# Order of work at the seams of a four-layer mixer kernel: output chunks one unit ahead, first scores inside the last projection unit, signals per bank

## Time and profile before

| | us |
|---|---|
| median of three runs | 2666.73 |
| profiled execution | 2667.27 |
| its span | 2665.3 |
| TensorE busy | 2569.6 (96%) |
| VectorE busy | 1645.6 (62%) |
| ScalarE busy | 1178.4 (44%) |
| GpSimd busy | 310.4 (12%) |
| mean granted TensorE clock | 0.989 of full speed |

### The profile page before, as it was taken

The page is one execution under the profiler, slowest core; times in us unless marked ns, Lnnn a source line. Parts: engine busy times, 40 slices in busy tenths (PEclk is TensorE's granted clock), DMA queues, the critical chain, the costliest instruction groups (busy, mean ns, idle before and its releaser), DMA issues.

```text
span 2665.3 us, 38269 instructions
## 1 busy us (share of the span) xinstructions
PE 2569.6 (96%) x13432; PEld 2165.7 (81%) x13432; DVE 1645.6 (62%) x2865; ACT 1178.4 (44%) x1819; POOL 310.4 (12%) x258
## 2 busy tenths in 40 slices
PE   8999999999999799999999899999999999999997
PEld 6889978888878577888878778888879998788886
DVE  7578567774252957667356667664375784776733
ACT  4367454443232745444235454442333773544421
POOL 1001121110010001111010021110010110211100
PEclk9999999999999999999999999999999999999999
DMA  4410023333233012332322023233333001233331
GB/s 157 135 33 1 1 95 103 94 96 101 74 112 96 9 56 81 101 95 79 114 73 72 32 80 102 95 94 97 98 97 112 14 2 40 80 102 96 94 98 53
DMA packets 61907, 210.90 MB, mean 79 GB/s; under 512 B 8528, under 2 KB 10320, under 8 KB 61776
## 3 DMA queue, kind: packets, MB, share of 16 engines
q1 hardware_dynamic: 61776, 209.13, 24.9%
HBM read 207.01 MB, written 2.10 MB: 78 GB/s over the span
## 4 chain that ended last, share of the span: by engine, by line
PE 86%; DVE 11%; ACT 1%; issue 1%; DMA 0%; DVEq 0%; SPq 0%; ACTq 0%
PE psum L304 20%; PE psum L305 20%; PE psum L306 20%; PE psum L1066 6%; PE psum L1056 3%; PE psum L902 2%; PE psum L904 2%; PE psum L903 2%; DVE left L1986 2%; PE psum L1046 2%; PE psum L1045 2%; DVE xl L477 2%; DVE h L494 1%; PE psum L338 1%; DVE share L1992 1%
## 5 line engine op out<-in xcount | busy, mean ns | idle before, releaser
L304 PE MATMUL psum<-xh,w_hi 128*128 128x512 f32 x1712 | 671.1, 392 | 18.2 <-DVE w_lo L266 13.5
L305 PE MATMUL psum<-xh,w_lo 128*128 128x512 f32 x1712 | 669.5, 391 | 0.0
L306 PE MATMUL psum<-xl,w_hi 128*128 128x512 f32 x1712 | 669.1, 391 | 0.0
L266 DVE TENSOR_TENSOR w_lo<-w_raw,w_hi 128x1024 fp32r<-128x1024 f32 x226 | 279.0, 1250 | 516.4 <-ACT w_hi L260 515.1
L260 ACT ACTIVATE w_hi<-w_raw 128x1024 fp32r<-128x1024 f32 x226 | 235.0, 1056 | 570.0 <-PE psum L306 448.7
L304 PEld LDWEIGHTS psum<-xh,w_hi 128*128 128x128 f32 x1712 | 323.4, 189 | 87.2 <-issue 14.6
L306 PEld LDWEIGHTS psum<-xl,w_hi 128*128 128x128 f32 x1712 | 323.5, 189 | 67.7
L305 PEld LDWEIGHTS psum<-xh,w_lo 128*128 128x128 f32 x1712 | 323.7, 189 | 66.8
L698 DVE TENSOR_TENSOR w_lo<-w_raw,w_hi 128x1024 fp32r<-128x1024 f32 x160 | 209.3, 1308 | 253.6 <-ACT w_hi L694 253.6
L304 PE MATMUL psum<-ah,w_hi 128*128 (+1 forms) x704 | 273.9, 389 | 0.0
L305 PE MATMUL psum<-ah,w_lo 128*128 (+1 forms) x704 | 273.9, 389 | 0.0
(11 more groups left out here) (197 smaller groups left out, 3836.7 us busy)
## 6 DMA issues: line engine op xcount, KB each, us to landing
w_raw<-w_up SPq DMA_DIRECT2D x176, 512.0 KB, 3.6
w_raw<-w_down SPq DMA_DIRECT2D x88, 512.0 KB, 3.6
w_raw<-nsa_in SPq DMA_DIRECT2D x56, 512.0 KB, 4.1
w_raw<-sb_in SPq DMA_DIRECT2D x24, 512.0 KB, 3.6
w_raw<-nsa_out SPq DMA_DIRECT2D x16, 512.0 KB, 3.6
w_raw<-swa_in SPq DMA_DIRECT2D x10, 512.0 KB, 3.9
w_raw<-sb_out SPq DMA_DIRECT2D x8, 512.0 KB, 3.6
w_raw<-swa_out SPq DMA_DIRECT2D x8, 512.0 KB, 3.6
```

Source lines behind the costliest of these rows:

```text
L266: nc.vector.tensor_tensor(w_lo[:, u % RING, :], w_raw[:, u % RING, :], w_hi[:, u % RING, :].bitcast(F32), ALU.subtract).then_inc(split_don ...
L304: nc.tensor.matmul(bank(p, o), wh[:, k, o, :], xhi(k), start=(first and k == 0), stop=False)
L305: nc.tensor.matmul(bank(p, o), wl[:, k, o, :], xhi(k), start=False, stop=False)
L306: mm = nc.tensor.matmul(bank(p, o), wh[:, k, o, :], xlo(k), start=False, stop=(last and k == 1))
```

## The change

1. In `dve_nsa`, the second flat subtraction moves behind two weight splits and the gate copy.
2. In `pe_nsa`, products and transposes of the compressed branch are placed anew between the window units; the first four scores stand in the middle of the last window unit. A new semaphore `wk_done` tells DVE when the window keys alone are whole. DVE copies them after the first four biased tiles, ACT the window values after the second exponential. All four query operands are made ahead on ACT.
3. In `pe_out`, chunks 4 and 5 are turned before unit 1, and 6 and 7 before unit 2; on ACT and DVE one weight split stands behind chunk 1 and one behind chunk 5 (nsa and swa).
4. In `pe_sb`, the scores of tiles 0 to 3 stand before the last value unit, whose products are ordered by bank; `sv_done` signals each bank, `sv_free` each copy of one; one weight split moves behind the sigmoids and scans of tiles 0 and 1.

```diff
@@ kv_panel
                     for o in range(2):
-                        three(bank(p, o), ...
+                        mm = three(bank(p, o), ...
+                    if keys is not None and c == DC - 1:
+                        mm.then_inc(keys, 1)
@@ dve_k
-            dve.wait_ge(units_done, u_end)
+            if b:
+                dve.wait_ge(wk_done, nsa_before[l] + 1)
+            else:
+                dve.wait_ge(units_done, u_end)
@@ pe_attention, values(s)
+                    if kind == "nsa" and it == 0 and s == 0:
+                        pe.wait_ge(evac_s, s_after[plan.mix_p[l] + 7])
@@ dve_attention, ahead()
                 queries(0, 1)
-                if late and kind == "nsa":
-                    late()
                 for s in range(4):
                     biased(0, s)
                 if kind == "nsa":
+                    late()
                     queries(0, 2)
@@ act_attention, turn() and ahead()
                     exps(s)
+                    if kind == "nsa" and it == 0 and s == 1:
+                        late()
...
-                queries(0, 0)
-                queries(0, 1)
-                if late and kind == "nsa":
-                    late()
-                    queries(0, 2)
-                    queries(0, 3)
+                for r in range(R if kind == "nsa" else 2):
+                    queries(0, r)
@@ act_turn_o (and the same with split_lo behind dve_turn_o in dve_nsa and dve_swa)
                 nc.scalar.activation(xh[:, c, :], turn_bank(l, c), ACT.Copy).then_inc(oh_done, 1)
+                if c in (1, 5):
+                    split_hi(act, plan.out_u[l] + c // 4 + AHEAD)
@@ pe_out
-                if j >= 2:
-                    pe_turn_o(pe, l, 2 * j)
-                    pe_turn_o(pe, l, 2 * j + 1)
+                if j < 3:
+                    pe_turn_o(pe, l, 2 * j + 2)
+                    pe_turn_o(pe, l, 2 * j + 3)
                 pe.wait_ge(o_ready, 8 * l + 2 * j + 2)
@@ act_out and dve_out (done = 2 in nsa and swa)
-            split_his(act, u, 6)
+            split_his(act, u + done, 6 - done)
@@ pe_nsa
-            window(2, turn_late)
-            mixed(0)
+            window(2, mix_first)          # mixed(0), turned(2), turned(3)
             mixed(1)
-            window(3, mix_late)
-            pe.wait_ge(co_ready, TC * (k + 1))
-            pe.wait_ge(k_ready, kr_before[l] + 2)
-            pe.wait_ge(v_ready, kvs_before[l] + 1)
-            ...
+            mixed(2)
+            mixed(3)
+
+            def last_unit(first_scores):
+                def begin():
+                    pe.wait_ge(co_ready, TC * (k + 1))
+                    pe.wait_ge(k_ready, kr_before[l] + 2)
+                    pe.wait_ge(v_ready, kvs_before[l] + 1)
+                    first_scores()
+
+                window(3, begin)
+                pe.wait_ge(evac_v, v_after[W + 1])
@@ act_nsa
-            split_his(act, u0 + 25, 3)
+            split_his(act, u0 + 25, 2)
             mixed(0)
-            mixed(1)
-            ...
+            split_hi(act, u0 + 27 + AHEAD)
+            for i in range(1, TC):
+                mixed(i)
+            act_attention(act, l, "nsa", lambda: act_v(act, ch, 1, p0 + 6, u0 + 28))
@@ dve_nsa
             low_flat(0)
+            split_lo(dve, u0 + 6 + AHEAD)
             dve_q(dve, ch, l, 0, p0 + 1, u0 + 8, -SCALE, qt)
-            low_flat(1)
-            split_lo(dve, u0 + 8 + AHEAD)
+            split_los(dve, u0 + 7, 2)
             dve.wait_ge(gate_sum, k + 1)
             nc.vector.tensor_tensor(glog[:], ...
+            low_flat(1)
@@ pe_sb
+            def value_unit(k, j):
+                u, last = u0 + 4 * k + j, (k, j) == (5, 3)
+                pe.wait_ge(split_done, u + 1)
+                order = [(q, t) for t in range(TC) for q in range(2)] if last else [(q, t) for q in range(2) for t in range(TC)]
+                for q, t in order:
+                    ...
+                    if last and q and t < TC - 1:
+                        mm.then_inc(sv_done, 1)
+                mm.then_inc(units_done, 1)
...
                 if s >= 2:
                     pe.wait_ge(wt_done, n0 + s - 1)
+                else:
+                    pe.wait_ge(sv_free, TC * sb_before[l] + s + 1)
...
             scores(0)
             scores(2)
-            panel_free(pe, p0 + 7)
+            value_unit(5, 3)
@@ act_sb, values(half) and after
+                    if half and t < TC - 1:
+                        act.wait_ge(sv_done, (TC - 1) * sb_before[l] + t + 1)
+                    elif half:
+                        act.wait_ge(units_done, u0 + 24)
...
             sigmoids(1)
+            split_hi(act, u0 + 23 + AHEAD)
             values(1)
@@ dve_sb
                 sticks(s)
+                if s == 1:
+                    split_lo(dve, u0 + 23 + AHEAD)
```

More of the change, by code:

```diff
@@ L823, in hybrid_layers @@
         k_ready = sem("k_ready")
+        wk_done = sem("wk_done")
         wkh_done = sem("wkh_done")
+        sv_done = sem("sv_done")
+        sv_free = sem("sv_free")
         wkx_done = sem("wkx_done")
@@ L921, in kv_panel @@
                     for o in range(2):
-                        three(bank(p, o), wh[:, k, o * P:(o + 1) * P], wl[:, k, o * P:(o + 1) * P],
-                              xh[:, c, :], xl[:, c, :], c == 0, c == DC - 1)
+                        mm = three(bank(p, o), wh[:, k, o * P:(o + 1) * P], wl[:, k, o * P:(o + 1) * P],
+                                   xh[:, c, :], xl[:, c, :], c == 0, c == DC - 1)
+                    if keys is not None and c == DC - 1:
+                        mm.then_inc(keys, 1)
                     for t in range(TC):
@@ L1361, in pe_out, with act_out @@
             pe_post(pe, 2 * l, p + 1)
-        def act_out(act, l):
+        def act_out(act, l, done=0):
             u = plan.out_u[l]
-            split_his(act, u, 6)
+            split_his(act, u + done, 6 - done)
             act_squares(act, 2 * l, 0, plan.out_p[l], u + 4)
@@ L1368, in act_out, with dve_out @@
             act_squares(act, 2 * l, 1, plan.out_p[l] + 1, u + 8)
-        def dve_out(dve, l):
+        def dve_out(dve, l, done=0):
             u = plan.out_u[l]
-            split_los(dve, u, 6)
+            split_los(dve, u + done, 6 - done)
             dve_take_u(dve, 2 * l, plan.out_p[l], mix_u)
@@ L1415, in window @@
             def window(j, halfway=None):
-                kv_panel(pe, W, [u0 + 24 + x for x in range(4)], (j,), halfway)
+                kv_panel(pe, W, [u0 + 24 + x for x in range(4)], (j,), halfway, wk_done)
             def cmp_scores(half):
@@ L1444, in mixed, with mix_first @@
                 mm.then_inc(co_done, 1)
-            def turn_late():
+            def mix_first():
+                mixed(0)
                 turned(2)
                 turned(3)
-            def mix_late():
-                mixed(2)
-                mixed(3)
             hidden(0)
@@ L1493, in pe_nsa @@
             turned(1)
[L1494 to L1495 removed]
+            window(2, mix_first)
             mixed(1)
[L1497 to L1506 removed]
+            mixed(2)
[8 more added lines that the diff above has]
+                pe.wait_ge(evac_v, v_after[W + 1])
+            pe_attention(pe, l, "nsa", last_unit)
             pe_out(pe, l)
@@ L1883, in values @@
                             mm.then_inc(spv_done, 1)
+            for k in range(4, 6):
+                panel_free(pe, p0 + k)
+                for j in range(4 if k == 4 else 3):
+                    value_unit(k, j)
+            panel_free(pe, p0 + 6)
+            pe.wait_ge(q_done, qn_before[l] + 4)
             scores(0)
             scores(2)
-            panel_free(pe, p0 + 7)
+            value_unit(5, 3)
             for s in range(0, SB_TILES, 2):
@@ L1908, in values @@
             def values(half):
-                act.wait_ge(units_done, u0 + 20 + 4 * half)
+                if half == 0:
+                    act.wait_ge(units_done, u0 + 20)
                 for t in range(TC):
-                    m = ch.then(nc.scalar.activation(sv_t[:, t, 512 * half:512 * half + 512], bank(p0 + 4 + half, t), ACT.Copy,
-                                                     scale=rt[:, t:t + 1]))
-                act.wait_ge(s_chain, m)
+                    if half and t < TC - 1:
+                        act.wait_ge(sv_done, (TC - 1) * sb_before[l] + t + 1)
+                    elif half:
+                        act.wait_ge(units_done, u0 + 24)
+                    x = nc.scalar.activation(sv_t[:, t, 512 * half:512 * half + 512], bank(p0 + 4 + half, t), ACT.Copy, scale=rt[:, t:t + 1])
+                    if half:
+                        x.then_inc(sv_free, 1)
+                    else:
+                        m = ch.then(x)
+                if half:
+                    act.wait_ge(sv_free, TC * (sb_before[l] + 1))
+                else:
+                    act.wait_ge(s_chain, m)
                 act.sem_inc(evac_s, 1)
```

47 lines of the change are left out of this document (15 added, 32 removed).

## The result

The changed kernel takes 2632.3 us (median of 4 runs, 2630.08 to 2634.34) against 2667.3 (4 runs beside it, 2664.41 to 2670.0): a ratio of 0.9869, 95% interval 0.9852 to 0.9886. The forecast was 2633.

What follows compares the result with a forecast made beforehand. TensorE, busy 96% of the span, was taken as the bound, with only standstill and low clock to gain. Terms 7.6 + 4.8 + 19.3 + 2.8 = 34.5 us off 2666.7 gave 2632.2, stated as 2633; range 2626 to 2645.

Steps and rivals of the forecast that it cites:

- the tails that I counted: Low clock behind stalls: 1.7 us at query units of layers 0 and 3, 2.8 at output projections of layers 2 and 3.
- rival B: Start of attention, layers 0 and 3: late value evacuation and key copies hold TensorE instead; gain 29.7 us, 2637; chance 0.11.
- the 3.03 us: TensorE's wait before the output projection's last chunk pair, laid to fourth-unit weight splits made only after all eight chunks.
- rival A: Stalls go, but low clock falls on moved seams in other places; gain 24.2 us, 2642.5; chance 0.14.
- C: Output projection: a split's wait holds chunks queued behind it on ACT, 1.57 + 3.03 returns; gain 15.2 us, 2651.5; chance 0.06.
- D: Slower: attention loop of both NSA layers starts with ACT behind and never catches up; 2670.6 at 0.6 us a group; chance 0.03.

Runs made afterwards that it cites:

- value_banks: Changed kernel with window values' first bank copied on ACT once whole and the first key twin two tiles later: 2631.40 us.
- late_splits: Changed kernel with all the output projection's weight splits behind chunk 8 again on ACT and DVE, chunks still turned early: 2632.49 us.
- sb_only: Kernel before with only the stick-breaking change (scores ahead of the last value unit, values copied bank by bank): 2662.78 us.
- flats_only: Kernel before with only two weight splits and the gate copy moved ahead of the second flat subtraction: 2662.15 us.
- before_shifted: Kernel before with layer 0's first row-sum product done three times, so everything behind comes some 1.7 us later: 2666.16 us.
- both_waits: value_banks plus the low part of output chunk 0 made one tile earlier on DVE in the nsa layers: 2629.43 us, ratio 0.9855.

## Why the prediction was right

**The sum.** Forecast 34.5 us, measured 35.0 in the medians and 37.2 in the spans. By part, forecast and measured: 7.6 and 7.6; 4.8 and 4.0; 19.3 and 20.9; 2.8 and 3.9. The mechanism of each part was right, but the sum is closer than its terms deserve: one is too high and two too low, and the tails that I counted were those of one profile. Executions of the kernel before spread from 2661.6 to 2670.6 us over all series.

**Part 1** held to the step: splits at 64.4, 0.1 us of TensorE's idle time left, the tail gone in both layers. But 7.6 us is its worth only where both stalls had a tail. Against the 108.9 us of the profiles in which a query stall had none, the gain is 2.1 us a layer.

**Part 2** held in kind. The start came out as laid down: in layer 3, which had no tail, the first transposes of attention come 2.55 us earlier, where I had 2.44 (2.74 less 0.3 for the key banks). What I had too low is the price at the first value products: from those transposes to the second group of value products 1.18 us is lost where I had 0.65. ScalarE's first copy cost 0.7 us where I had 0.4, since it began 0.25 us behind the evacuation and not at once; the third exponential cost 0.1 where I had 0.25. These two idle times are 0.77 us, and value_banks, which has neither, is 1.01 us faster over the same stretch, so the rest is no idle time: 0.24 us of it goes with the stall, as in part 3, and 0.17 stays open. The 1.0 us a layer is all of rival B that is true.

**Part 3** was low by 1.6 us: 20.9 against 19.3. In layer 0, where no tail is in play, the stalls are 4.60 and the gain is 5.16. Without a stall the transposes' end and the next unit's start overlap (318.31 to 319.34 against 319.10), with one they do not: some 0.25 us each time. I took the idle time for the whole price. The tails were right in this profile (2.7 us in layer 2 and in layer 3, none in layer 0). The reason that I gave for the 3.03 us, the splits' place, holds for the kernel before, where it makes 1.46 of them. In the changed kernel it is not needed: late_splits loses nothing by late splits. My own layout (copies through at 328.5, the reader at 332) had said so.

**Part 4**: 2.6 us at the third scan against 2.8. TensorE itself had waited longer there before:

```profile
PE psum L1865 <- ACTq L1914: 3.7, 1, 3.7
```

That wait is gone, and the gain is still VectorE's 2.6 us, which bears out that VectorE paces this loop. The rest of the 3.9 was no part of the sum: 1.6 us because no low clock met the out projection of layer 1, which is luck, less 0.4 us lost in the loop. That loss is 0.4 to 1.5 us over the kernels that have part 4, and sb_only and value_banks pay it on top of a tail at the out projection.

**The low clock.** I let the tails come or go by 3 us at the seams that stay. At the seams around the feed-forward parts they cost nothing: this one has low clock in the changed kernel and had none before, and both take 28.4 us from mark to mark, as TensorE waits there for ScalarE and VectorE in any case (it is busy for 3.15 of the 5 us in the first row). It answers to the earlier trace rows:

```profile
720.00:725.00 5.00, 3.15 (x17) 0.84 0.92 332
...
725.00:730.00 5.00, 5.00 (x22) 0.82 0.09 37
```

They cost where TensorE sets the pace. Of rival A one half is right (flats_only and before_shifted show tails that come at an untouched stall) and the other is not: with no stall over 1 us left in the out projections of layers 0, 2 and 3, none of the six kernels profiled with early turns has a tail there. The three together take 151.1 us in five of those six, 149.6 in both_waits, and 172.0 to 172.6 in the six with the old order, wherever its tails fell, while part 1 alone showed 5.1 of 7.5. C did not show: the rows of part 3 have both splits without idle time before them, and the chunk copies wait for TensorE's transposes alone. Nor did D: from the second group of value products to the last one of layer 3 it is 134.4 us before and after.

The Trainium skill, "TensorE: Matmul & The Clock Gate", "Part 1: The HAM clock gate (the "warmup" mystery)", has windows that run free of the kernel. That equal stalls get unequal tails when the work is shifted agrees with it, and so does the spread of executions of one program (2661.9 to 2669.9 us at clocks of 0.993 to 0.989). That two profiles of that program repeated every tail is not what I had read into it; why they did was not shown.

## What to carry to other kernels

An in-order queue that serves TensorE should hold first what TensorE needs first; where a weight split is late, look at what stands ahead of it before moving it, since here turning chunks one unit earlier cured the split's lateness as well. Copies of a panel that are released bank by bank were worth 1.7 us in one place and, with a copy moved, 1.0 in another, wherever the next work on the same engine stands behind them. Measure such edits by marks inside the trace. In layers 0, 2 and 3 and in the feed-forward parts, stretches with no stall of 2 us or more in them repeated to some 0.1 us; a stretch that keeps such a stall moves by up to 2.8 us with its tail, and the stick-breaking mixer moved by 2.5 us in kernels that have all of part 4, so look at the granted clock before calling a difference a gain. The totals of one kernel moved by up to 9 us.

## What the runs showed of the hardware

- One of five executions of the changed kernel in the last series took 5169.88 us, 1.96 times the others. Its trace has a granted clock of 1.000 throughout, yet TensorE's busy time is 5130.1 us, and a 512-column product takes 675 ns instead of 390:

```profile
core 0: 5167.9 us, clock 1.000
```

```profile
L304 PE MATMUL psum<-xh,w_hi 128*128 128x512 f32 x1712 | 1155.2, 675 | 0.0
```

  The other engines were busy for about as long as usual (VectorE 1654.0 us, ScalarE 1192.0 us). Where the low clock is recorded, as behind the 3.03 us stall of layer 2 before, such a product starts every 0.43 us and lasts 0.63; here one starts every 0.44 to 0.56 us. What slowed TensorE is open; the clock column does not show it.
- A tail of low clock cost 1.2 to 2.8 us behind a stall of 2.2 to 3.0 us, or nothing: the same stalls had none in other profiles. Two stalls of 1.57 us, 6.6 us apart, had none in any of three layers (one profile).
- A profile with 1.7 us of added work near the start had a span 1.1 us shorter, because both query tails and parts of two others were missing and one new one came; without any edit, executions of the kernel before differ by more.
